# Feed-forward gate and up steps of a two-block transformer kernel: order of the products inside a half step

## The chip, the cores and the metric

The kernel runs on one core of a Trainium2 chip. The time is device microseconds (us) of one execution. Three runs of the kernel before gave 1703.51, 1703.61 and 1705.5 us, median 1703.61 us.

## The reference

The input x has 256 tokens of width 1024. It goes through nine phases: feed-forward, mixer, feed-forward (first block), then twice feed-forward, mixer, feed-forward (second block, two layers). The change touches the feed-forward phases alone, of which there are six. Each computes, in float32,

```
h = rms_norm(x, g)                       # 256 x 1024
a = silu(h @ w_gate) * (h @ w_up)        # 256 x 2816 each
x = x + 0.5 * (a @ w_down)               # in two of the six with an rms_norm around a @ w_down
```

The mixers are attention blocks of several kinds with their own projections.

## The kernel before, in words

Full float32 accuracy is reached with float32r products on TensorE (PE): every operand v is split into `hi` (v rounded to float32r) and `lo` (v - hi), and a product is taken as hi*hi + hi*lo + lo*hi. ScalarE (ACT) makes `w_hi` from the loaded weights `raw` (L265), VectorE (DVE) makes `w_lo` (L272). Weights come in units of 128 x 2048 numbers (1 MB); there are three `raw` buffers and four `w_hi`/`w_lo` pairs. PE counts used units in `unit_used`, and ACT waits for it before it overwrites a pair.

A feed-forward phase has 11 steps of 256 hidden columns (`STEP_F`). Step 0 is done in another layout (`pe_gate_up_part`). Steps 1 to 10 call `pe_gate_up` and then the down product:

- `pe_gate_up` (its products on L589 and L593) computes the transposed gate and up values of the step in four PSUM banks, j = 0 to 3: gate and up of the first 128 hidden columns, gate and up of the second 128. It has two half steps (`kh` 0 and 1), one weight unit each, each for four of the eight 128-row chunks of the width 1024. In a half step, bank by bank, it does four products of 512 columns (weights hi; the moving operand is hi and lo of h side by side, 2 x 256 tokens, L589), then four of 256 columns (weights lo, moving hi of h, added into the first 256 columns of the bank, L593). So a half step has 16 + 16 products, a step 32 + 32. At the end of a bank's last product in the second half step, PE signals `gu_done` for j = 0, 1, 2; for j = 3 the signal is `unit_used`.
- `pe_down` (L635 to L637, in `pe_rows`) multiplies the activations of the step before by the down weights: two token tiles of 12 products of 512 columns each, accumulating in banks 0 to 3. It waits for `act_lo_ready` of the step before.

`pe_gate_up` of a step begins with a wait for `gu_summed`: all four banks of the step before must have been read by DVE, since all steps from 2 on use the same banks 4 to 7.

DVE does per step, strictly in this order (`dve_step`): w_lo of two units (L272); then `gate(0)`: a reduce that adds the two halves of bank 0 (L783, after `gu_done`) and a multiply by the row scale (L789); then w_lo of a third unit, `split(3)`; then `up(0)`: reduce of bank 1 (L783) and multiply by the silu result (L794); `gate(1)`: bank 2 (L783, L789); `lo(0)`: low part of the activations (L798); `up(1)`: bank 3 (L783, L794); `lo(1)` (L798). In the last step the third split stands behind `lo(1)`. In step 1 it stands behind `up(0)`. ACT does the three w_hi, and between the DVE operations the silu (L742) and the high part of the activations (L746).

Steps 2 to 9 are a loop of two turns of four steps. After step 10's `pe_gate_up`, `pe_last_rows` does the down products of steps 9 and 10 token tile by token tile: tile 0 with step 9's activations (12 products), tile 0 with step 10's (`before_second` waits for the last `act_lo_ready` of the phase), then tile 1 of both. In it PE also transposes x for the next phase (L365), after DVE's residual (L418, or L426 and L435).

Of the kernel before, what the change touches and what calls it, by code (L numbers as in the profile page):

```python
# [25 lines left out]
P = 128  # L26
# [3 lines left out]
KC = D // P  # L30
DFF = 2816
STEP_F = 256
# [73 lines left out]
def build(nc, A, place, out):  # L106

    with ExitStack() as ctx:
# [7 lines left out]
        def sb(name, shape, dt=F32):  # L116
            return ctx.enter_context(nc.sbuf_tensor(name, shape, dt))
# [5 lines left out]
        aT = sb("aT", [P, 2, KC, S], F32R)  # L123
# [43 lines left out]
            return ps[:, 4 + t, 0:2 * P].rearrange("p (f s) -> p f s", f=2)  # L167

        RSTD_BANK = 0

        def gu_bank(s, j):

            return ps[:, (4 + j) if s != 1 else (2, 3, 6, 7)[j], :].rearrange("p (w s) -> p w s", w=2)
# [124 lines left out]
        def rstd(ph, t):  # L298
            return column(ph["pre_c"][t])
# [59 lines left out]
        def wait_rstd(eng, ph, t):  # L359
            eng.wait_ge(rstd_ready, ph["pre_c"][t] + 1)  # L360
# [213 lines left out]
        def pe_gate_up(pe, ph, s, like, between=None):  # L574


            u0, n0 = ph["u0"], ph["n0"]
            if like != 1:
                pe.wait_ge(gu_summed, 4 * s + 4 * n0)
            for kh in range(2):  # L580
                d = kh - 1
                pe.wait_ge(lo_ready, 3 * s + (u0 + d + 1))
                slot = (3 * like + u0 + d) % W_SLOTS
                hi, lo = (w.rearrange("p (k f) -> p k f", k=KC // 2) for w in (w_hi[slot][:, :], w_lo[slot][:, :]))
                for j, c in enumerate((0, STEP_F, P, STEP_F + P)):
                    dst = gu_bank(like, j)
                    for k in range(KC // 2):
                        a = kh * (KC // 2) + k
                        nc.tensor.matmul(dst, hi[:, k, c:c + P], aT[:, :, a, :], start=a == 0, stop=a == KC - 1,  # L589
                                         skip_group_check=True)  # L590
                    for k in range(KC // 2):
                        a = kh * (KC // 2) + k
                        mm = nc.tensor.matmul(dst[:, 0, :], lo[:, k, c:c + P], aT_hi[:, a, :], start=False,  # L593
                                              stop=a == KC - 1, skip_group_check=True)
                    if kh == 1 and j < 3:
                        mm.then_inc(gu_done, 1)
                mm.then_inc(unit_used, 1)
                if kh == 0 and between:
                    between()
# [15 lines left out]
        def pe_rstd_rows(pe, ph):  # L615
            for t in range(NT):
                wait_rstd(pe, ph, t)
                last = nc.tensor.transpose(ps[:, RSTD_BANK, t * P:(t + 1) * P],
                                           rstd(ph, t).broadcast_to([P, P]), ident)
# [68 lines left out]
        def pe_ffn(pe, ph):  # L688
            u0, s0, last = ph["u0"], ph["s0"], STEPS - 1

            def part(kh, t, between=None):
                mm = pe_gate_up_part(pe, ph, t, kh, between)
                if t == 1:
                    mm.then_inc(unit_used, 1)
                elif kh == 1:
                    mm.then_inc(gu_t0_done, 1)
            pe_enter(pe, ph, part)

            def first_acts():
                for t in range(NT):  # L700
                    pe_act_transposes(pe, ph, t)
                pe_rstd_rows(pe, ph)
            pe_gate_up(pe, ph, 1, 1, between=first_acts)
            pe_down(pe, ph, 1, 1, first=True)
            with pe.Fori(2, last, 4) as s:
                for j in range(4):
                    pe_gate_up(pe, ph, s + j, 2 + j)
                    pe_down(pe, ph, s + j, 2 + j)
            pe_gate_up(pe, ph, last, last)

            def before_first():
                pe.wait_ge(act_lo_ready, 2 * (last + s0))

            def before_second():
                pe.wait_ge(act_lo_ready, 2 * (last + s0) + 2)
            pe_last_rows(pe, ph, [(act_hi[1], act_lo[1]), (act_hi[0], act_lo[0])],
                         before=(before_first, before_second), ffn_end=2 * (last + s0) + 2)

        def act_step(act, ph, s, like, in_loop=False, last=False):
            u0, s0, par = ph["u0"], ph["s0"], like % 2  # L720

            def split(d):
                n = 3 * s + (u0 + d)
                if in_loop:
                    turn = (u0 + d - (u0 + d) % RAW_SLOTS) // RAW_SLOTS
                    split_hi(act, n, like=3 * like + u0 + d, loads=s + turn + 1)
                else:
                    split_hi(act, n)
# [19 lines left out]
            if like == 1:  # L748
# [4 lines left out]
                act.wait_ge(rstd_rows_done, ph["ffn_before"] + 1)  # L753
                nc.scalar.activation(rstd_rows, ps[:, RSTD_BANK, 0:S], ACT.Copy).then_inc(rstd_rows_ready, 1)
            split(2)
# [1806 lines left out]
```

## Time and profile before

| | |
|---|---|
| median of 3 runs | 1703.61 us (1703.51 to 1705.5) |
| profiled execution, first to last instruction (span) | 1701.3 us |
| PE busy | 1688.0 us, 99% |
| weight loads busy (PEld) | 1398.8 us, 82% |
| DVE busy | 1228.3 us, 72% |
| ACT busy | 865.5 us, 51% |
| chain that ended last | PE 95%, DVE 3% |
| DMA, mean over the span | 176 GB/s |
| granted TensorE clock | 1.000, its upper level (2.4 GHz) |

The page gives the profiled execution's time as its span; the runs' median lies 2.3 us above it, which is what lies before the first and behind the last instruction. PE, PEld, DVE and ACT stand for TensorE's products, its weight loads, VectorE and ScalarE. Products are pipelined and their ends are modelled, so the length of a product is read from start to start of neighbours, not from its duration. A timeline row is: start in us from the span's start, length in us, engine, line, operation, output<-input, shapes, how many were merged; in brackets the idle time before it and what ended it.

### The profile page before, as it was taken

What the parts mean: (1) busy time and instruction counts of PE and PEld (TensorE: products, weight loads), DVE (VectorE), ACT (ScalarE), POOL (GpSimd) and SP (SyncE); (2) the same over time, 40 slices, a digit from 0 to 9 for tenths busy, and PEclk for the clock granted to TensorE, in tenths of its full rate; (3) what the DMA queues carried; (4) which work ended last, traced back from release to release, by engine and by line L of the source; (5) the groups of instructions that cost most, each with busy time, mean ns of one, the idle gap of its engine ahead of it and who ended that gap; (6) DMA issues with size and microseconds to landing.
All of it is one profiled execution on the core that took longest, in us unless ns stands there. A gap on an engine that the chain in (4) does not pass through costs nothing.

```text
span 1701.3 us, 24131 instructions
## 1 busy us (share of the span) xinstructions
PE 1688.0 (99%) x9040; PEld 1398.8 (82%) x9040; DVE 1228.3 (72%) x1841; ACT 865.5 (51%) x1108; POOL 107.3 (6%) x141
## 2 busy tenths in 40 slices
PE   8999999999999999999999999999999999999999
PEld 6888887788888888878778888888888787788887
DVE  6776756776777776769866767776767698667675
ACT  5444565644445444566664444454445666644442
POOL 2000100200002000110011000020001010110000
PEclk9999999999999999999999999999999999999999
DMA  8655442465447645534344655475455344346452
GB/s 302 203 175 201 158 171 100 165 219 192 179 173 244 208 173 198 174 109 159 130 134 170 216 184 186 173 248 201 176 198 173 103 158 137 128 172 219 179 192 74
DMA packets 69812, 299.95 MB, mean 176 GB/s; under 512 B 5408, under 2 KB 7680, under 8 KB 44512
## 3 DMA queue, kind: packets, MB, share of 16 engines
q1 hardware_dynamic: 66752, 291.52, 49.0%
q0 software_dynamic: 2688, 7.19, 1.7%
q8 instruction: 55, 0.90, 0.2%
q14 instruction: 29, 0.24, 0.0%
q10 hardware_dynamic: 288, 0.10, 0.0%
HBM read 297.74 MB, written 1.05 MB: 176 GB/s over the span
## 4 chain that ended last, share of the span: by engine, by line
PE 95%; DVE 3%; ACT 1%; issue 1%; DMA 0%; POOL 0%; ACTq 0%; DVEq 0%
PE ps L589 25%; PE ps L593 13%; PE ps L635 9%; PE ps L636 8%; PE ps L637 8%; PE ps L870 6%; PE ps L872 6%; PE ps L871 6%; PE ps L564 2%; PE ps L565 2%; PE ps L960 1%; PE ps L1038 1%; PE ps L567 1%; PE ps L365 1%; PE ps L571 1%; DVE w_lo L272 1%
## 5 line engine op out<-in xcount | busy, mean ns | idle before, releaser
L272 DVE TENSOR_TENSOR w_lo<-raw,w_hi 128x2048 fp32r<-128x2048 f32 x275 | 627.6, 2292 | 144.9 <-ACT w_hi L265 143.9
L265 ACT ACTIVATE w_hi<-raw 128x2048 fp32r<-128x2048 f32 x275 | 524.9, 1914 | 258.4 <-PE ps L593 181.6
L589 PE MATMUL ps<-aT,w_hi 128*128 128x512 f32 x1920 | 523.8, 394 | 0.8
L589 PEld LDWEIGHTS ps<-aT,w_hi 128*128 128x128 f32 x1920 | 331.8, 189 | 50.6 <-issue 3.3
L593 PEld LDWEIGHTS ps<-aT,w_lo 128*128 128x128 f32 x1920 | 294.3, 189 | 40.5
L593 PE MATMUL ps<-aT,w_lo 128*128 128x256 f32 x1920 | 305.1, 281 | 0.0
L783 DVE TENSOR_REDUCE tmp<-ps 128x256 f32<-128x512 f32 x240 | 164.6, 686 | 134.3 <-PE ps L593 134.3
L635 PE MATMUL ps<-w_hi,act_hi 128*128 128x512 f32 x576 | 226.0, 392 | 0.1
L636 PE MATMUL ps<-w_lo,act_hi 128*128 128x512 f32 x576 | 225.3, 391 | 0.0
L637 PE MATMUL ps<-w_hi,act_lo 128*128 128x512 f32 x576 | 225.2, 391 | 0.0
L870 PE MATMUL ps<-w_hi,aT 128*128 128x512 f32 (+1 forms) x432 | 174.3, 404 | 0.0
L872 PE MATMUL ps<-w_hi,aT 128*128 128x512 f32 (+1 forms) x432 | 165.5, 383 | 0.0
L871 PE MATMUL ps<-w_lo,aT 128*128 128x512 f32 (+1 forms) x432 | 165.3, 383 | 0.0
L746 ACT ACTIVATE act_hi<-tmp 128x256 fp32r<-128x256 f32 x120 | 50.3, 419 | 214.0 <-DVE tmp L794 214.0
L635 PEld LDWEIGHTS ps<-w_hi,act_hi 128*128 128x128 f32 x576 | 108.2, 188 | 23.2 <-issue 1.4
L637 PEld LDWEIGHTS ps<-w_hi,act_lo 128*128 128x128 f32 x576 | 108.1, 188 | 23.2
L636 PEld LDWEIGHTS ps<-w_lo,act_hi 128*128 128x128 f32 x576 | 108.2, 188 | 20.8
L870 PEld LDWEIGHTS ps<-w_hi,aT 128*128 128x128 f32 x432 | 81.2, 188 | 28.1 <-issue 12.3
L742 ACT ACTIVATE tmp<-tmp 128x256 f32<-128x256 f32 x120 | 50.4, 420 | 105.6 <-DVE tmp L789 105.6
L872 PEld LDWEIGHTS ps<-w_hi,aT 128*128 128x128 f32 x432 | 81.2, 188 | 16.7
L871 PEld LDWEIGHTS ps<-w_lo,aT 128*128 128x128 f32 x432 | 81.4, 189 | 12.9
L798 DVE TENSOR_TENSOR act_lo<-tmp,act_hi 128x256 fp32r<-128x256 f32 x120 | 50.6, 422 | 29.1 <-ACT act_hi L746 29.1
(303 smaller groups left out, 1569.2 us busy)
## 6 DMA issues: line engine op xcount, KB each, us to landing
raw<-in_ffn_units SPq DMA_DIRECT2D x197, 1024.0 KB, 5.0
raw<-in_w_in SPq DMA_DIRECT2D x34, 1024.0 KB, 5.3
raw<-in_w_gate SPq DMA_DIRECT2D x24, 1024.0 KB, 5.1
raw<-in_w_out SPq DMA_DIRECT2D x12, 1024.0 KB, 4.9
qk_t<-in_nsa_cmp_w POOLq DMA_DIRECT2D x8, 512.0 KB, 5.9
raw<-in_w_br_b SPq DMA_DIRECT2D x4, 1024.0 KB, 4.9
raw<-in_w_br_a SPq DMA_DIRECT2D x2, 1024.0 KB, 4.8
raw<-in_w_br_c SPq DMA_DIRECT2D x2, 1024.0 KB, 4.8
```

The source lines that it names most:

```text
L265: nc.scalar.activation(w_hi[w][:, :], raw[k][:, :], ACT.Copy).then_inc(hi_ready, 1)
L272: nc.vector.tensor_tensor(w_lo[w][:, :], raw[k][:, :], w_hi[w][:, :].bitcast(F32), ALU.subtract)\
L589: nc.tensor.matmul(dst, hi[:, k, c:c + P], aT[:, :, a, :], start=a == 0, stop=a == KC - 1, skip_group_check=True)
L593: mm = nc.tensor.matmul(dst[:, 0, :], lo[:, k, c:c + P], aT_hi[:, a, :], start=False, stop=a == KC - 1, skip_group_check=True)
L635: nc.tensor.matmul(dst, hi_a[:, c, toks], hi[:, c, cols], start=first and c == 0, stop=False)
L636: nc.tensor.matmul(dst, hi_a[:, c, toks], lo[:, c, cols], start=False, stop=False)
L637: mm = nc.tensor.matmul(dst, lo_a[:, c, toks], hi[:, c, cols], start=False, stop=last and c == 1)
L783: nc.vector.tensor_reduce(dst[:, f, :], bank.rearrange("p w s -> p s w"), AX.X, ALU.add)\
L798: nc.vector.tensor_tensor(act_lo[par][:, f, :], up_t[:, f, :], act_hi[par][:, f, :].bitcast(F32), ALU.subtract).then_inc(act_lo_ready, 1)
L870: nc.tensor.matmul(dst, aT_hi[:, a, toks], hi[:, k, :], start=a == 0, stop=False)
L871: nc.tensor.matmul(dst, aT_hi[:, a, toks], lo[:, k, :], start=False, stop=False)
L872: last = nc.tensor.matmul(dst, aT_lo[:, a, toks], hi[:, k, :], start=False, stop=a == KC - 1)
```

## The change

In each half step all sixteen 512-column products come first (bank 0, 1, 2, 3), then all sixteen 256-column products (bank 0, 1, 2, 3). The signals stay on the same product of each bank, the last 256-column one. Nothing else moves; the number of instructions of each kind is the same.

```diff
         RSTD_BANK = 0
+        GU_COLS = (0, STEP_F, P, STEP_F + P)
...
                 hi, lo = (w.rearrange("p (k f) -> p k f", k=KC // 2) for w in (w_hi[slot][:, :], w_lo[slot][:, :]))
-                for j, c in enumerate((0, STEP_F, P, STEP_F + P)):
-                    dst = gu_bank(like, j)
+                for j, c in enumerate(GU_COLS):
                     for k in range(KC // 2):
                         a = kh * (KC // 2) + k
-                        nc.tensor.matmul(dst, hi[:, k, c:c + P], aT[:, :, a, :], start=a == 0, stop=a == KC - 1,
-                                         skip_group_check=True)
+                        nc.tensor.matmul(gu_bank(like, j), hi[:, k, c:c + P], aT[:, :, a, :], start=a == 0,
+                                         stop=a == KC - 1, skip_group_check=True)
+                for j, c in enumerate(GU_COLS):
+                    dst = gu_bank(like, j)
                     for k in range(KC // 2):
                         a = kh * (KC // 2) + k
                         mm = nc.tensor.matmul(dst[:, 0, :], lo[:, k, c:c + P], aT_hi[:, a, :], start=False,
                                               stop=a == KC - 1, skip_group_check=True)
                     if kh == 1 and j < 3:
                         mm.then_inc(gu_done, 1)
```

## Rows read from the trace of the kernel before

**Rows 1.** The page: busy time of the engines; weight loads (count, size, us to landing).
```profile
PE 1688.0 (99%) x9040; PEld 1398.8 (82%) x9040; DVE 1228.3 (72%) x1841; ACT 865.5 (51%) x1108; POOL 107.3 (6%) x141
...
raw<-in_ffn_units SPq DMA_DIRECT2D x197, 1024.0 KB, 5.0
```

**Rows 2.** Timeline, PE, first half step of a step that begins at 73.69.
```profile
73.69 1.07 PE L589 MATMUL ps<-aT,w_hi 128*128 128x512 f32 x4
74.60 0.64 PE L593 MATMUL ps<-aT,w_lo 128*128 128x256 f32 x4
75.07 1.09 PE L589 MATMUL ps<-aT,w_hi 128*128 128x512 f32 x4
76.00 0.63 PE L593 MATMUL ps<-aT,w_lo 128*128 128x256 f32 x4
...
79.28 1.09 PE L589 MATMUL ps<-aT,w_hi 128*128 128x512 f32 x4
```

**Rows 3.** Timeline, PE, down product before it: products 1, 10 and 22 of 24.
```profile
68.20 0.40 PE L635 MATMUL ps<-w_hi,act_hi 128*128 128x512 f32 x1
...
70.29 0.39 PE L635 MATMUL ps<-w_hi,act_hi 128*128 128x512 f32 x1
...
73.01 0.39 PE L635 MATMUL ps<-w_hi,act_hi 128*128 128x512 f32 x1
```

**Rows 4.** Timeline, PE, a mixer's unbroken run of 256-column products: two, 45 starts apart.
```profile
764.68 0.28 PE L872 MATMUL ps<-w_hi,aT 128*128 128x256 f32 x1
...
770.08 0.28 PE L872 MATMUL ps<-w_hi,aT 128*128 128x256 f32 x1
```

**Rows 5.** Timeline, all engines, loop step that begins at 57.01: signal of bank 0, then DVE.
```profile
57.01 1.07 PE L589 MATMUL ps<-aT,w_hi 128*128 128x512 f32 x4
...
64.00 1.09 PE L589 MATMUL ps<-aT,w_hi 128*128 128x512 f32 x4
64.20 0.69 DVE L783 TENSOR_REDUCE tmp<-ps 128x256 f32<-128x512 f32 x1 [2.42 <-PE ps L593]
65.27 2.29 DVE L272 TENSOR_TENSOR w_lo<-raw,w_hi 128x2048 fp32r<-128x2048 f32 x1
67.47 0.68 DVE L783 TENSOR_REDUCE tmp<-ps 128x256 f32<-128x512 f32 x1
70.02 0.68 DVE L783 TENSOR_REDUCE tmp<-ps 128x256 f32<-128x512 f32 x1
71.74 0.43 DVE L798 TENSOR_TENSOR act_lo<-tmp,act_hi 128x256 fp32r<-128x256 f32 x1 [0.49 <-ACT act_hi L746]
```

**Rows 6.** Timeline, end of the first feed-forward phase: step 10, then the last rows.
```profile
173.81 1.07 PE L589 MATMUL ps<-aT,w_hi 128*128 128x512 f32 x4
...
185.01 0.40 PE L635 MATMUL ps<-w_hi,act_hi 128*128 128x512 f32 x1
...
186.85 0.43 DVE L798 TENSOR_TENSOR act_lo<-tmp,act_hi 128x256 fp32r<-128x256 f32 x1 [0.48 <-ACT act_hi L746]
...
187.78 0.39 PE L635 MATMUL ps<-w_hi,act_hi 128*128 128x512 f32 x1
```

**Rows 7.** Timeline, step 1 to step 2 of the second feed-forward phase.
```profile
338.33 1.17 PE L589 MATMUL ps<-aT,w_hi 128*128 128x512 f32 x4
...
343.22 0.68 DVE L783 TENSOR_REDUCE tmp<-ps 128x256 f32<-128x512 f32 x1
...
348.94 0.68 DVE L783 TENSOR_REDUCE tmp<-ps 128x256 f32<-128x512 f32 x1
...
349.76 1.19 PE L589 MATMUL ps<-aT,w_hi 128*128 128x512 f32 x4
```

**Rows 8.** Timeline, end of the third feed-forward phase: DVE's residual, PE's transposes for the next.
```profile
687.16 1.40 DVE L418 SCALAR_TENSOR_TENSOR x<-ps,stats,x 128x512 f32<-128x512 f32 x2
688.78 1.04 PE L365 MATMUL ps<-consts,x 128*128 128x128 f32 x8
```

**Rows 9.** A boundary at which PE idles: window, us, busy by engine, PEclk, DMA share, GB/s.
```profile
315.50:318.50 3.00, 1.72 (x10) 0.98 (x8) 2.56 (x4) 1.09 (x4) 0.88 (x2) 1.00 0.60 167
```

## The prediction

> **What bounds the kernel now.** I read first the busy shares and the chain that ended last: PE is busy 99% of the span [rows 1], and the chain is PE's nearly throughout. So two things count: how fast PE streams its products, and whether the change makes it wait. For the stream I read PE's timeline through a step, start to start. For the waits I read DVE's timeline of a step, and for each result that PE needs from DVE how long it has been ready. There are six feed-forward phases, each with steps 1 to 10 of gate and up, 60 steps; eight per phase (2 to 9) lie inside the loop, 48 in all.
>
> The stream: after a long run of 512-column products four of them take 74.60 - 73.69 = 0.91 us, 0.227 each; after 256-column ones four take 76.00 - 75.07 = 0.93, 0.232 each. Four 256-column ones take 75.07 - 74.60 = 0.47 [rows 2]. In the down product behind a step the first nine products still need 70.29 - 68.20 = 2.09 us (0.232 each), the next twelve 73.01 - 70.29 = 2.72 (0.227 each) [rows 3]. So 512-column products are slow by 0.005 us each for about nine after 256-column ones, then recover. In a long run of 256-column products each takes 5.40/45 = 0.120 us [rows 4], a little more than 0.47/4.
>
> The waits: a step begins at 57.01, the next at 73.69, period 16.69 (steps repeat to 0.01). Bank 0 is complete when the next bank's products start at 64.00; its reduce starts at 64.20, 7.19 after the step's start. The fourth reduce ends at 70.02 + 0.68 = 70.70 [rows 5], and the next step may then begin: it does so at 73.69 [rows 2], 2.99 us later. That is the cover of the wait at the head of `pe_gate_up`.
>
> **Part 1, the stream.** The counts stay, only the order changes. First half step: sixteen 512-column products behind the down product's, 16 x 0.227 = 3.63; sixteen 256-column, 0.47 for the first four and 12 x 0.120 = 1.44, 1.91. Sum 5.54, now 79.28 - 73.69 = 5.59 [rows 2]. Second: nine slow 512-column products 2.09, seven at 0.227 1.59, then 1.91: 5.59. Sum 11.13, now 185.01 - 173.81 = 11.20 [rows 6]; gain 0.07 us a step, if PE never waits: 60 x 0.07 = 4.2 us. Bounds: if 256-column products keep 0.1175 the step is 0.06 shorter still; if the slow rate lasts for all sixteen of the second half step it is 0.04 longer.
>
> The Trainium skill ("TensorE: Matmul & The Clock Gate", section "Wait — 56ns, not 53.3ns?") says that start to start a product costs its columns at the clock and a small fixed amount, so that the order would be free. The trace disagrees in size, with 0.227 and 0.232 us for the same 512 columns. By that rule, with the steps as long as now, Part 1 gains nothing and the later signals below come 0.1 us later: my estimate of the whole would be 1718.4 us in place of 1714.5.
>
> **Part 2, the signals come later.** Bank 0's signal now comes after 5.59 + 1.40 = 6.99 us of a step. New: 5.54 + 3.68 (the sixteen) + 0.47 = 9.69; with the same 0.20 us to the reduce, DVE starts at 9.89, 2.70 later. The four signals then follow every 0.48 us in place of 1.40, which DVE can't use: its order is serial and in the loop step it already runs without a pause from the first reduce on. From first reduce to end of the fourth it needs 70.70 - 64.20 = 6.50 [rows 5], the third weight split among it. So the banks are free at 9.89 + 6.50 = 16.39.
>
> How long from there to PE's first product? The trace has this wait six times, at step 1 to 2: the fourth reduce ends at 348.94 + 0.68 = 349.62, the group of four starts at 349.76 and is 1.19 long, against 1.07 for one that starts unhindered, so it runs as if begun at 349.88 [rows 2, 7]: 0.25 us. So the next step can begin at 16.64, against 11.13 + 5.49 (the down product) = 16.62 by the stream. The cover of 2.99 us is spent, by a hair more than all. PE's queue then runs empty each step, and I charge the first half step the slow start of nine products, 0.04: period 16.39 + 0.04 + 0.25 = 16.68. Against 16.69 that gains 0.01 a step, 48 x 0.01 = 0.5 us. Bounds: the wait is missed and the stream's 0.07 stays, -3.4 us; or the DVE chain or the wake-up is 0.1 longer, +4.3 us. I take the middle since each of its terms has a row.
>
> Behind the waiting PE instruction only its own products are queued. On DVE, the splits of the next step start 2.7 later; they are needed by PE only in the next half steps, more than 9 us on. The raw buffers come free 2.7 later as well; their loads (5.0 us to land [rows 1]) end some 4 us ahead of ACT's use. Nothing charged for these.
>
> **Part 3, the last step of a phase.** Here the activations are needed at once: PE does twelve products (185.01 to 187.78, 2.77 us), then waits in `before_second` for the last low part. Now it ends at 186.85 + 0.43 = 187.28, just ahead of 187.78 [rows 6]. In the new order the last step has no split in the chain: 65.27 - 64.20 = 1.07, then from 67.47 to 71.74 + 0.43, 4.70, together 5.77 [rows 5]. End at 9.89 + 5.77 = 15.66; PE resumes 0.25 later at 15.91. By the stream it would have been there at 11.13 + 2.77 = 13.90, so it stands idle for 2.0 us; against now (187.78 - 173.81 = 13.97) it is 1.94 late. Six phases: 6 x 1.94 = 11.6 us. Bounds: the wake-up 0.15 and 0.35 with a slow restart, 10.8 to 12.6.
>
> Does the boundary take it back? All that follows waits for PE's own results, so it moves along. DVE's end moves by 15.66 - 13.48 = 2.2, PE by 1.94: where DVE's residual follows its splits, its two halves end at 687.9 and 688.56 and PE's transposes start at 688.78 [rows 8], the second four of them 0.4 later. The margin shrinks by 0.25 and holds. Charged nothing; if gone, a few tenths at three boundaries.
>
> **Part 4, step 1.** Here the first reduce is held by a split, not by the signal: it starts at 343.22, and the new signal would let it start at 342.76 (second half begun at 338.33 [rows 7], 4.43 on by the same sums). So the step 1 to 2 wait stays, the first half step gives 0.03: 6 x 0.03 = 0.2 us.
>
> **Sum.** -0.5 - 0.2 + 11.6 = +10.9 us: span 1701.3 to 1712.2. The runs' median lies 2.3 above the span, 1703.6, so 1714.5 us, +0.64%.
>
> **Rivals.**
> (a) The stream wins: PE is 99% busy, the reordering takes 4.2 us out of it, and the later signals hide: 1699.4 us. For it speaks that today no wait of this kind lasts in the loop. Against it: in the last step `lo(1)` would have to end by about 13.65 of the step, and the chain of DVE and ACT operations, each behind the other, gives 15.66. Decided there, at `before_second`. 5%.
> (b) The waits are absorbed elsewhere, or the change does less than it says, and the two effects cancel: 1703.6. For: PE waits a little at some boundaries, [rows 9] shows 1.3 us idle in one. Against: what it waits for there starts from PE's own last product. 7%.
> (c) The loop steps are held harder than the hair above, by 0.3 us each (DVE's chain stretched, or a load that lands late and holds a split before the first reduce): 48 x 0.3 = 14.4 more, 1729. For: the cover is at zero, every delay now shows. Against: DVE's operations keep their durations from step to step, and loads have 4 us. 8%.
> (d) The clock falls in the 2 us pauses. The trace shows 1.00 through 1.3 us idle [rows 9], and no idle time of 2.0 under way. If the twenty-four products after the pause (5.5 us) ran at half rate: 6 x 5.5 = 33 more, 1747. The Trainium skill (same page, section "A second HAM failure mode: psum-queue depth-cycling") says that short idles between groups of products can make the clock swing between its levels; this trace does not show it, with 1.00 throughout. 2%.
>
> **The numbers.** The forecast, 78%: both waits as summed. Its bounds are -3.4 - 0.2 + 10.8 = +7.2 and +4.3 - 0.2 + 12.6 = +16.7: 1710.8 to 1720.3. The range 1709.5 to 1721 holds that and a little more. About 0.2%, 3.4 us, is what a measurement can tell from no change. Faster by more: 5%, from (a). Within: 7%, from (b). Slower by more: the rest, 88%.
>
> **What would show it.** In the profile after: 256-column runs of sixteen 1.91 long; first reduce 9.9 us into a loop step; the fourth ending 0.25 before the next step's first product; period 16.68. In the last step PE idle about 2.0 us ahead of L635 with DVE's L798 as what ended it, six times, 12 us in PE's waits, where now this wait does not appear. The clock 1.00. The prediction is wrong if L798 of the last step ends within 2.8 us after the last gate and up product, or if loop steps differ from 16.68 by over 0.1.

## The result and the profile after

The changed kernel takes 1711.47 us (median of 4 runs, 1711.11 to 1711.89), against 1703.68 us before: ratio 1.0048, 95% interval 1.0035 to 1.006. It is 7.8 us slower; 10.9 was forecast. The profiled execution's span is 1709.8 us, its own time 1711.89 us.

Busy times and the waits of PE, from the page and from the table of waits of the changed kernel (engine, line, who was waited for: us in total, times, longest):

```profile
PE 1687.6 (99%) x9040; PEld 1398.0 (82%) x9040; DVE 1223.9 (72%) x1841; ACT 860.1 (50%) x1108; POOL 107.8 (6%) x141
```

```profile
PE ps L637 <- DVE act_lo L800: 9.3, 6, 1.6
PE ps L366 <- DMA consts<-in_const_table: 4.0, 1, 4.0
PE ps L366 <- DMA x<-in_x: 2.0, 1, 2.0
PE ps L366 <- DVE x L436: 1.3, 1, 1.3
```

Work is what it was (against [rows 1]), so the difference is idle time and stream. The first row is new: six times PE's down product (L637, before L635) waits for the last low part. The other three rows stand in the table of the kernel before too, with 4.3, 1.6 and 1.3 us. (Lines behind the change are 1 or 2 higher than before. In the experiments with `bank_runs` they are higher still: the two kinds of gate and up products are L596 and L603, the down product is L645 to L647, the low part L808.)

A loop step of the changed kernel on PE and DVE, from its timeline, and the start of the next:

```profile
57.38 3.86 PE L589 MATMUL ps<-aT,w_hi 128*128 128x512 f32 x16
61.09 2.08 PE L595 MATMUL ps<-aT,w_lo 128*128 128x256 f32 x16
63.00 3.82 PE L589 MATMUL ps<-aT,w_hi 128*128 128x512 f32 x16
66.65 2.08 PE L595 MATMUL ps<-aT,w_lo 128*128 128x256 f32 x16
67.33 0.69 DVE L785 TENSOR_REDUCE tmp<-ps 128x256 f32<-128x512 f32 x1 [2.39 <-PE ps L595]
68.39 2.29 DVE L273 TENSOR_TENSOR w_lo<-raw,w_hi 128x2048 fp32r<-128x2048 f32 x1
...
73.14 0.68 DVE L785 TENSOR_REDUCE tmp<-ps 128x256 f32<-128x512 f32 x1
73.95 0.43 DVE L796 TENSOR_TENSOR tmp<-tmp 128x256 f32<-128x256 f32 x1
...
74.03 3.87 PE L589 MATMUL ps<-aT,w_hi 128*128 128x512 f32 x16
```

The first reduce is 67.33 - 57.38 = 9.95 us into the step, where [rows 5] had 7.19. The fourth ends at 73.14 + 0.68 = 73.82, 0.21 before the next step at 74.03, where [rows 5] and [rows 2] had 2.99. Period 74.03 - 57.38 = 16.65 against 16.69. The steps shown lie in the first phase; in the other phases most are 16.63 (418.36 to 434.99, for one). The table of waits shows no row for this, since the idle time is small and the first products' recorded starts hide it; it is read from the group's length, 3.86 or 3.87 in place of 3.79 for the same sixteen products where nothing holds them (e4_bank_waits, below). From start to start the group takes 61.09 - 57.38 = 3.71, where 3.63 is what it takes unhindered.

The end of the first feed-forward phase, against [rows 6]:

```profile
173.94 3.83 PE L589 MATMUL ps<-aT,w_hi 128*128 128x512 f32 x16
...
185.09 0.40 PE L637 MATMUL ps<-w_hi,act_hi 128*128 128x512 f32 x1
...
187.61 0.39 PE L639 MATMUL ps<-w_hi,act_lo 128*128 128x512 f32 x1
189.54 0.50 PE L637 MATMUL ps<-w_hi,act_hi 128*128 128x512 f32 x1 [1.55 <-DVE act_lo L800]
...
190.36 0.40 PE L637 MATMUL ps<-w_hi,act_hi 128*128 128x512 f32 x1
```

```profile
183.91 0.69 DVE L785 TENSOR_REDUCE tmp<-ps 128x256 f32<-128x512 f32 x1 [2.85 <-PE ps L595]
...
187.44 0.68 DVE L785 TENSOR_REDUCE tmp<-ps 128x256 f32<-128x512 f32 x1
188.16 0.42 DVE L796 TENSOR_TENSOR tmp<-tmp 128x256 f32<-128x256 f32 x1
189.07 0.42 DVE L800 TENSOR_TENSOR act_lo<-tmp,act_hi 128x256 fp32r<-128x256 f32 x1 [0.48 <-ACT act_hi L748]
```

DVE finishes the last low part at 189.49 and PE goes on at 189.54. From the step's start that is 15.60 us, against 187.78 - 173.81 = 13.97 in [rows 6]: 1.63 us later by the starts. The next three products take 190.36 - 189.54 = 0.82 us, against 3 x 0.227 = 0.68 in a run, so the restart costs another 0.14, 1.77 in all.

### The profile page after: what moved, and what is told of

Its sections match the earlier page's. It is cut to its first block, busy times and chain, and to the rows that moved or that the text cites. A ratio compares the mean times of both kernels' runs of the same rounds, so it can differ in the third digit from the quotient of the medians.

```text
span 1709.8 us, 24131 instructions
## 1 busy us (share of the span) xinstructions
PE 1687.6 (99%) x9040; PEld 1398.0 (82%) x9040; DVE 1223.9 (72%) x1841; ACT 860.1 (50%) x1108; POOL 107.8 (6%) x141
## 3 DMA queue, kind: packets, MB, share of 16 engines
q0 software_dynamic: 2688, 7.19, 1.6%
## 4 chain that ended last, share of the span: by engine, by line
PE 94%; DVE 5%; ACT 1%; issue 0%; DMA 0%; POOL 0%; DVEq 0%; ACTq 0%
PE ps L589 26%; PE ps L595 13%; PE ps L637 8%; PE ps L638 8%; PE ps L639 8%; PE ps L872 6%; PE ps L874 6%; PE ps L873 6%; PE ps L565 2%; PE ps L566 2%; DVE tmp L785 2%; PE ps L962 1%; PE ps L1040 1%; DVE w_lo L273 1%; PE ps L572 1%; PE ps L568 1%
## 5 line engine op out<-in xcount | busy, mean ns | idle before, releaser
L266 ACT ACTIVATE w_hi<-raw 128x2048 fp32r<-128x2048 f32 x275 | 519.5, 1911 | 133.0 <-PE ps L595 72.6
L589 PE MATMUL ps<-aT,w_hi 128*128 128x512 f32 x1920 | 460.7, 392 | 0.8
L589 PEld LDWEIGHTS ps<-aT,w_hi 128*128 128x128 f32 x1920 | 352.7, 188 | 81.2 <-issue 11.1
L595 PEld LDWEIGHTS ps<-aT,w_lo 128*128 128x128 f32 x1920 | 246.2, 191 | 9.4
L595 PE MATMUL ps<-aT,w_lo 128*128 128x256 f32 x1920 | 249.1, 283 | 0.0
L637 PE MATMUL ps<-w_hi,act_hi 128*128 128x512 f32 x576 | 227.1, 394 | 9.4 <-DVE act_lo L800 9.3
L637 PEld LDWEIGHTS ps<-w_hi,act_hi 128*128 128x128 f32 x576 | 108.4, 188 | 34.7 <-DVE act_lo L800 11.9
L639 PEld LDWEIGHTS ps<-w_hi,act_lo 128*128 128x128 f32 x576 | 108.2, 188 | 23.2
L874 PEld LDWEIGHTS ps<-w_hi,aT 128*128 128x128 f32 x432 | 81.2, 188 | 16.8
L800 DVE TENSOR_TENSOR act_lo<-tmp,act_hi 128x256 fp32r<-128x256 f32 x120 | 50.6, 422 | 29.1 <-ACT act_hi L748 29.1
```

The source lines that it names most:

```text
L266: nc.scalar.activation(w_hi[w][:, :], raw[k][:, :], ACT.Copy).then_inc(hi_ready, 1)
L589: nc.tensor.matmul(gu_bank(like, j), hi[:, k, c:c + P], aT[:, :, a, :], start=a == 0, stop=a == KC - 1, skip_group_check=True)
L637: nc.tensor.matmul(dst, hi_a[:, c, toks], hi[:, c, cols], start=first and c == 0, stop=False)
L639: mm = nc.tensor.matmul(dst, lo_a[:, c, toks], hi[:, c, cols], start=False, stop=last and c == 1)
L800: nc.vector.tensor_tensor(act_lo[par][:, f, :], up_t[:, f, :], act_hi[par][:, f, :].bitcast(F32), ALU.subtract).then_inc(act_lo_ready, 1)
L874: last = nc.tensor.matmul(dst, aT_lo[:, a, toks], hi[:, k, :], start=False, stop=a == KC - 1)
```

## The experiments

All are edits of the changed kernel; e8_old_order_bank_waits gives it back the order of before. `EACH` stands for the order of before (bank by bank), `ALL` for the new order, `PAIRS` for two banks at a time. Medians of the kernel before in these sessions were 1703.2 to 1703.6 us.

**e1_last_old and e2_only_last: the end of a phase and the loop, apart.**

```diff
+            return EACH if like == STEPS - 1 else ALL
```

is e1_last_old, and e2_only_last is

```diff
+            return ALL if like == STEPS - 1 else EACH
```

> New order in steps 1 to 9, the order of before in step 10 of each feed-forward phase. Theory A (the whole loss is PE's wait for the last activations at the end of a phase, 1.7 us six times; the loop steps gain): the end is as before, the eight loop steps keep 16.64 against 16.69 us, so 48 x 0.045 = 2.2 us less than before, 1701.5 us. Rival B (the boundary loses because the splits and loads behind the loop come later, whatever the last step does): about 1708 to 1711 us, slower than before.

> The order of before in steps 1 to 9, the new order in step 10 alone. Theory A: loop steps at 16.69 us, six ends 1.7 us later than before, 1703.7 + 10.4 = 1714 us, slower than the changed kernel by the 2.2 us that its loop gains. Rival B: near 1703.7 us, since the loop's signals are as before.

Measured: e1_last_old 1700.27 us (ratio to before 0.9982, 0.9973 to 0.9991), e2_only_last 1713.80 us (1.0059, 1.0045 to 1.0072). Six uses of the new order in step 10 cost 10.3 us, more than the whole loss; nine steps of it per phase gain 3.3 us, where 2.2 was expected: in the traces the six loops (start of step 2 to start of step 10) take 798.6 us in sum against 801.5, 2.9 less, and step 1's first half step, left out of the expectation, gives 0.3. Together they would give 1703.5 + 10.3 - 3.3 = 1710.5, measured 1711.5. The two do not add up exactly: the loops of the changed kernel take 799.2 us, 0.6 more than those of e1_last_old, for a reason not found; the rest is no more than the spread of e1_last_old's runs, 1699.9 to 1701.6. In e2_only_last the waits are those of the changed kernel:

```profile
PE ps L645 <- DVE act_lo L808: 9.3, 6, 1.6
```

and in e1_last_old there is none on a low part. Rival B, a boundary that loses because the loop's splits and loads come later, is out: with the loop's signals late and step 10 as before, the kernel is faster than before.

**e3_first_half: the new order where no signal moves.**

```diff
+            return ALL if kh == 0 else EACH
```

> New order in the first half step alone, the order of before in the second, so every signal to VectorE stays where it was. Theory A: no wait is added, sixteen 512-column products in a row lose the slow start behind 256-column ones: first half step 5.54 in place of 5.59 us, 60 x 0.047 = 2.8 us less, 1700.9 us. Rival C (the order of products is free, and what the loop gained came from elsewhere): 1703.7 us.

Measured: 1699.64 us (0.9975, 0.9966 to 0.9985), 3.9 us under before where 2.8 was expected. The order is not free. Its timeline:

```profile
57.03 3.79 PE L596 MATMUL ps<-aT,w_hi 128*128 128x512 f32 x16
60.66 2.08 PE L603 MATMUL ps<-aT,w_lo 128*128 128x256 f32 x16
62.57 1.09 PE L596 MATMUL ps<-aT,w_hi 128*128 128x512 f32 x4
63.50 0.63 PE L603 MATMUL ps<-aT,w_lo 128*128 128x256 f32 x4
...
68.18 0.40 PE L645 MATMUL ps<-w_hi,act_hi 128*128 128x512 f32 x1
...
70.25 0.39 PE L645 MATMUL ps<-w_hi,act_hi 128*128 128x512 f32 x1
...
73.65 0.61 PE L596 MATMUL ps<-aT,w_hi 128*128 128x512 f32 x2
```

The first half step takes 62.57 - 57.03 = 5.54 us (5.59 in [rows 2]), as summed, the period 73.65 - 57.03 = 16.62. Sixty steps at 0.07 would be 4.2 us; 3.9 were measured. The 0.02 of a step that the expectation left out is in the down product, whose first nine products take 70.25 - 68.18 = 2.07 us, 2.09 in [rows 3].

**e4_bank_waits: the wait at the head of the step, taken apart.** Ahead of each bank's first product PE waits for that bank's reduce alone; step 10 in the old order as in e1_last_old.

```diff
-            if like != 1:
-                pe.wait_ge(gu_summed, 4 * s + 4 * n0)
...
+                        if kh == 0 and like != 1:
+                            pe.wait_ge(gu_summed, 4 * s + (4 * n0 - 3 + j))
```

> As e1_last_old, and the one wait for four read banks at the head of a step is split into one wait ahead of each bank's first product. Theory A: bank 3's first product is 2.7 us into the step, so the wait that held the loop steps at 16.64 us is covered, and they run at the stream's 16.62: about 48 x 0.02 = 1.0 us under e1_last_old, 1700.4 us. Rival D (the loop steps are not held by this wait but by what the products themselves take): same as e1_last_old; four waits on PE's queue could cost a few hundredths each, then slower.

Measured: 1694.92 us (0.9949, 0.9936 to 0.9963), 5.35 us under e1_last_old where 1.0 was expected. Its timeline:

```profile
56.42 3.79 PE L596 MATMUL ps<-aT,w_hi 128*128 128x512 f32 x16
60.05 2.08 PE L603 MATMUL ps<-aT,w_lo 128*128 128x256 f32 x16
61.96 3.82 PE L596 MATMUL ps<-aT,w_hi 128*128 128x512 f32 x16
65.61 2.08 PE L603 MATMUL ps<-aT,w_lo 128*128 128x256 f32 x16
...
67.53 0.40 PE L645 MATMUL ps<-w_hi,act_hi 128*128 128x512 f32 x1
...
68.69 0.39 PE L647 MATMUL ps<-w_hi,act_lo 128*128 128x512 f32 x1
...
69.59 0.39 PE L645 MATMUL ps<-w_hi,act_hi 128*128 128x512 f32 x1
...
73.00 0.39 PE L596 MATMUL ps<-aT,w_hi 128*128 128x512 f32 x1
```

Two things had been left out of the expectation. The free-running step is 73.00 - 56.42 = 16.58 us, not 16.62: the sixteen products of the second half step take 65.61 - 61.96 = 3.65 and the first nine of the down product 69.59 - 67.53 = 2.06, where 3.68 and 2.09 [rows 3] were used. The slow start is shorter than in the kernel before. And the wait from step 1 to step 2, which [rows 7] shows in the kernel before, goes too. The loop steps of e1_last_old are 16.61 to 16.65 us long, most of them 16.63, so 48 x 0.05 = 2.4 us are the loop's. The rest, 2.9 us, is put down to that wait; e8_old_order_bank_waits, next, measures it alone at 2.6.

**e8_old_order_bank_waits: the waits of e4_bank_waits with the order of before throughout.**

```diff
+            return EACH
```

> The order of before throughout, with the wait at the head of a step split into one per bank. It tells how much of e4_bank_waits is the wait's split and how much the order. Theory A: in the kernel before only the wait from step 1 to step 2 lasts (0.3 us, six times), so 1703.5 - 1.9 = 1701.6 us; the rest of what e4_bank_waits gained (6.7 us) is the order's. Rival D (the split itself speeds the loop): well under 1700 us.

Measured: 1701.00 us (0.9985, 0.9976 to 0.9994): 2.6 us for the split wait alone, 6.1 us of e4_bank_waits' 8.6 for the order that it lets run free. The 2.6, not 1.9, is because the wait from step 1 to step 2 costs 0.4 us each time and not 0.3: step 2 begins 0.29 earlier, and its first half step, which no longer starts behind a wait, is another 0.11 shorter.

**e6_split_moved: the chain shortened instead of the wait.** DVE's third split of a loop step goes behind `lo(1)`.

```diff
             gate(0)
-            if like != 1 and not last:
-                split(3)
             up(0)
...
             lo(1)
+            if like != 1:
+                split(3)
             if last:
-                split(3)
                 split_lo(dve, ph["u_end"] + 1)
```

> The changed kernel; VectorE's third weight split of a loop step stands behind its last low part instead of between the first and the second bank. Theory A (the loop steps are held at 16.64 us by the wait for four read banks, because the chain with the split in it ends at 16.43): the chain ends at 14.2, the wait is covered, steps run at the stream's 16.573 us as in e4_bank_waits: 48 x 0.067 = 3.2 us less, 1708.3 us. Rival D (what e4_bank_waits gained, the loop gained by something else in it, such as its waits' place in PE's queue): 1711.5 us.

Measured: 1708.12 us (1.0027, 1.0017 to 1.0036), 3.4 us under the changed kernel; 3.2 was expected. Its timeline:

```profile
56.86 3.79 PE L589 MATMUL ps<-aT,w_hi 128*128 128x512 f32 x16
...
66.73 0.69 DVE L785 TENSOR_REDUCE tmp<-ps 128x256 f32<-128x512 f32 x1 [4.21 <-PE ps L595]
...
70.34 0.69 DVE L785 TENSOR_REDUCE tmp<-ps 128x256 f32<-128x512 f32 x1
...
73.44 0.84 PE L589 MATMUL ps<-aT,w_hi 128*128 128x512 f32 x3
```

The fourth reduce ends at 71.03, 2.4 us ahead of the next step, and the period is 73.44 - 56.86 = 16.58, as in e4_bank_waits. Two edits that share nothing but the cover of this wait give the same step; rival D of this run and of e4_bank_waits is out.

**e7_pairs: shorter runs in the second half step of steps 1 to 9.**

```diff
+            return ALL if kh == 0 else EACH if like == STEPS - 1 else PAIRS
```

> New order in the first half step; in the second half step of steps 1 to 9 banks 0 and 1 (eight and eight products), then banks 2 and 3; step 10's second half as before; one wait at the head. Theory A: the slow start is five to six 512-column products long behind a 256-column run of eight or sixteen, so the step is 16.59 us against 16.62 in e3_first_half; bank 0's signal comes at 7.9 us, the fourth reduce ends at 14.6, no wait: 48 x 0.03 = 1.4 us under e3_first_half, 1698.2 us. If the slow start is nine products long each time, 16.62 and 1699.6 us.

Measured: 1698.28 us (0.9966, 0.9954 to 0.9979), as expected for the short slow start, and not 1699.6. The period of a loop step is 16.59 us. Its timeline:

```profile
62.57 2.00 PE L596 MATMUL ps<-aT,w_hi 128*128 128x512 f32 x8
64.41 1.11 PE L603 MATMUL ps<-aT,w_lo 128*128 128x256 f32 x8
65.36 2.00 PE L596 MATMUL ps<-aT,w_hi 128*128 128x512 f32 x8
67.20 1.12 PE L603 MATMUL ps<-aT,w_lo 128*128 128x256 f32 x8
```

The first pair of banks of the second half step takes 65.36 - 62.57 = 2.79 us; two banks of the old order take twice 1.40 to 1.41, 2.81. Eight 512-column products behind eight 256-column ones take 1.84, against 1.82 at 0.227: the slow start costs about 0.02 us for each change from 256 to 512 columns, whether four, eight or sixteen 256-column products came before.

**e5_end_by_column: cover for the wait at the end.** In token tile 0 of step 10's rows, the products with the first 128 hidden columns come first and wait for the first low part only.

```diff
+        def pe_rows_by_column(pe, n, slot, hi_a, lo_a, ready):
...
+            for c in range(2):
+                if c:
+                    pe.wait_ge(act_lo_ready, ready)
+                for h in range(2):
...
+                    if t == 0 and final and ffn_end:
+                        mm = pe_rows_by_column(pe, n + i, (n + i) % W_SLOTS, hi_a, lo_a, ffn_end)
+                        continue
...
             def before_second():
-                pe.wait_ge(act_lo_ready, 2 * (last + s0) + 2)
+                pe.wait_ge(act_lo_ready, 2 * (last + s0) + 1)
```

> The changed kernel; at the end of a phase, in token tile 0 of step 10's down rows, the six products with the first 128 hidden columns come first and need only the first low part, the other six wait for the last. Theory A (PE's wait there is all that the ends lose): six products, 1.37 us, move ahead of the wait at each of six ends, 8.2 us less than the changed kernel, 1703.3 us. Rival E (VectorE is late as a whole at the phase's end: behind its last low part it makes two splits of 4.4 us before the residual that PE's transposes need, so PE waits there next, by about 1.1 us at the boundaries): most of it is given back, 1706 to 1709 us, and a wait of L366 for the residual of x appears.

Measured: 1708.18 us (1.0026, 1.0016 to 1.0036), 3.3 us under the changed kernel, not 8.2: rival E. Its table of waits:

```profile
PE ps L366 <- DVE x L436: 2.5, 3, 1.3
PE ps L366 <- DVE x L419: 2.2, 3, 0.7
...
PE ps L654 <- DVE act_lo L819: 1.2, 6, 0.2
```

and the end of the third phase in its timeline:

```profile
686.22 4.49 DVE L273 TENSOR_TENSOR w_lo<-raw,w_hi 128x2048 fp32r<-128x2048 f32 x2
690.62 1.40 DVE L419 SCALAR_TENSOR_TENSOR x<-ps,stats,x 128x512 f32<-128x512 f32 x2
```

```profile
691.51 1.22 PE L366 MATMUL ps<-consts,x 128*128 128x128 f32 x8 [0.74 <-DVE x L419]
```

The wait for the low part falls from 9.3 to 1.2 us, and the transposes now wait for the residual, 2.2 + 2.5 us where 1.3 was. DVE's two splits stand right ahead of that residual. So the delay at a phase's end is DVE's as a whole; PE moved forward meets it one stop later. The last phase, which no other follows and which has no such transposes, shows it from the other side: its end is 1.3 us shorter than in the changed kernel (27.3 to 25.9 us from the start of step 10), all that was expected, and the other five gain 0.2 to 0.6 each.

**e9_combined: the version that the runs point to, with the waits of e4_bank_waits.**

```diff
+            return EACH if like == STEPS - 1 and kh == 1 else ALL
```

> The version the runs point to: new order in all half steps but the second one of step 10, one wait per bank. Theory A: as e4_bank_waits, and step 10's first half step 0.05 us shorter at six phases: 1694.9 - 0.3 = 1694.6 us, loop steps 16.573 us, no wait of PE for the last low part. Rival: the split waits or step 10's order cost something at the boundary, then 1695 us or more; the two can be told apart only in the trace, by step 10's length of 11.15 against 11.20 us.

Measured: 1694.68 us (0.9951, 0.9937 to 0.9965), 8.6 us faster than before in the same session and 16.8 under the changed kernel. The 0.24 us under e4_bank_waits is within the spread of the runs; the trace has step 10's second half step begun after 177.83 - 172.29 = 5.54 us, as the sum says:

```profile
172.29 3.79 PE L596 MATMUL ps<-aT,w_hi 128*128 128x512 f32 x16
175.92 2.08 PE L603 MATMUL ps<-aT,w_lo 128*128 128x256 f32 x16
177.83 1.09 PE L596 MATMUL ps<-aT,w_hi 128*128 128x512 f32 x4
```

## Why the prediction was right, and where it was off

Way, size and range held: 1714.5 forecast with 1709.5 to 1721, 1711.5 measured. The slowdown was put at 10.9 us and is 7.8; the terms were off by about 3 us together, both large ones on the same side. The two profiled executions differ by 8.5: in them the six loops take 799.2 us against 801.5 (2.3 less, 0.5 forecast), step 1 gives 0.3 (0.2 forecast), and the six stretches from the start of a step 10 to the next phase, or to the end, are 10.7 longer (11.6 forecast). Another 0.5 lies ahead of the first gate and up product (23.11 against 22.61 us); in all eleven profiles this start lies between 22.4 and 23.2, whatever the order, so it is not the change's. By its own parts:

**Part 1, the stream.** The first half step was put at 5.54 and took 61.96 - 56.42 = 5.54 in e4_bank_waits. The second was put at 5.59 with nine slow products; it took 5.57 (61.96 to 67.53), and the first nine products of the down product 0.03 less than before. So the slow start of nine products, read from a place with eight runs of four ahead of it, was too long for one run of sixteen: there it is over after five (67.53 to 68.69 is 1.16 us, 0.232 each; 68.69 to 69.59 is 0.90 for four, the quick rate). The free step is 16.58, not 16.62. The gain open to the order was 0.11 us a step, not 0.07.

**Part 2, the later signals.** Right in mechanism: the first reduce comes 2.7 to 2.8 us later, the serial chain behind it is unchanged (73.82 - 67.33 = 6.49 against 6.50), and the cover is spent; e4_bank_waits and e6_split_moved show that this wait holds the loop at 16.63 to 16.65 in place of 16.58. Two small terms of the sum were mis-sized. The sixteen 512-column products of the second half step were put at 3.68 and took 66.65 - 63.00 = 3.65, for the reason given in Part 1. And the restart behind the wait was put at 0.25 + 0.04, although the 0.25, worked out from a group of four that was 0.12 longer than an unhindered one, already held the delay of the first products. Measured in whole, from the end of the fourth reduce to the next step as if begun unhindered, it is 0.21 + (3.71 - 3.63) = 0.29 in the step shown, where the two terms hold together, but 0.26 in most steps, those of period 16.63. So the loop gained 0.05 us a step instead of 0.01, and the steps before step 10 gain 2.3 us by the medians (e2_only_last less the changed kernel) where 0.7 was summed.

**Part 3, the end of a phase.** Right in mechanism and place: the row that was announced, L800 holding the down product six times, is there, and e1_last_old and e2_only_last put the whole loss on it. Mis-sized: 1.94 us forecast, 1.63 measured by the starts, 1.77 with the slow restart (10.3 us over six phases in e2_only_last, against 11.6). All three terms came from rows of the loop, for a place outside it. The term that failed most is the chain from first reduce to last low part: 189.49 - 183.91 = 5.58 us, not 5.77. From reduce to the multiply of `up` it is 188.16 - 187.44 = 0.72 here and 0.81 in the loop (73.95 - 73.14), and the chain has this twice; in step 1, outside the loop as well, it is 0.72 too. The way back from L800 to PE is 0.05 to the first product and 0.14 for the restart, 0.19 where 0.25 was put (in the loop 0.26 to 0.29). Against these goes the first reduce, 183.91 - 173.94 = 9.97 us into the step where 9.89 was summed: step 10 of the kernel before already has it at 7.26 (181.07 - 173.81) and not at the 7.19 of the loop. So rows of the loop are wrong here in both directions. That the loop's waits are against a register's value, and those of step 10 against a constant, is a guess at the shorter times; it was not tried apart.

That the boundary would give nothing back was right for the changed kernel. The margin of DVE's residual was charged at nothing; e5_end_by_column shows how thin it is.

**Part 4, step 1**, held: its wait stayed, and e4_bank_waits and e8_old_order_bank_waits remove it. One sum in it does not come out: with the terms shown, 3.68 + 0.47 + 0.20, the signal would let the reduce start after 4.35 us and not 4.43, at 342.68. The split holds it until 343.22 either way.

**The page on the fixed cost.** The Trainium skill ("TensorE: Matmul & The Clock Gate", section "Wait — 56ns, not 53.3ns?") gives each product its columns at the clock and a small fixed cost, by which the order would be free; the whole was put at 1718.4 us by it. e3_first_half, with no wait moved, is 3.9 us faster than before: rows and runs decide against it here.

**Rivals.** (a), the stream wins, falls on step 10 above all: with that step left as before the kernel is 3.3 us faster than before (e1_last_old), against the 4.2 of the rival. A smaller part falls on the loop's wait, about 3 us (e6_split_moved). (b) and (c) did not come. (d): PE's pauses are 1.94 us from start to start (187.61 to 189.54 for the first), and the granted clock is 1.00 in a window around each of the six, as in the stretch 184 to 194 us of the changed kernel (window, us, busy by engine, PEclk, DMA share, GB/s):

```profile
184.00:194.00 10.00, 8.45 (x42) 6.83 (x41) 9.38 (x13) 5.04 (x9) 0.48 (x1) 1.00 0.31 98
```

## What to carry to other kernels

When an order of work is changed on the engine that bounds a kernel, write down for each signal in it how much later it comes and how long its result has been ready today; the change is paid where that cover is shortest, here in one step of eleven, where the last low part had 0.5 us of cover and came 2.1 us later. Follow the delay through to the result that is waited for: the first signal comes 2.7 us later, the last low part only 2.1, since the new signals follow each other faster than the chain behind them and no longer hold it. Then apply the order where the cover is long and keep the old one at the edges, and split a wait for several buffers into one per buffer before judging the order. Take durations from the place that the sum is about: here the loop's rows were 0.19 us too long for the chain of step 10 and 0.07 too short for its first reduce.

## What the runs showed of the hardware that was not expected

Products of 512 columns, 0.227 us apart in a long run, are 0.232 apart for a few behind 256-column ones, and it does not matter much how many of these there were. Behind sixteen 256-column products this slow start is five products long (e4_bank_waits), and the first nine products of the down product take 2.06 us; in e3_first_half, where four runs of four stand ahead, they take 2.07, no more than rounding apart. In the kernel before, with eight runs of four ahead, the same nine take 2.09 [rows 3]; what is different there was not found, nor what the engine catches up on. A change of the weights' tile alone does not bring it: in the down product `w_hi` and `w_lo` alternate at 0.227.

Counted by changes from 256 to 512 columns in a step, the cost is about 0.02 us each, and this describes all orders that ran: 8 changes and a free step of 16.69 us (before), 5 and 16.62 (e3_first_half), 3 and 16.59 (e7_pairs), 2 and 16.58 (e4_bank_waits).
